# A 2-layer hybrid decoder step on one core: seven-product up-projection in the last chunk of each MLP too, and the last LayerNorm's first half shared with GpSimd

## The reference, cut to what matters

```python
D_MODEL = 1024; D_FF = 4 * D_MODEL
def layer_norm(x, g, b):
    mu = jnp.mean(x, axis=-1, keepdims=True)
    var = jnp.mean(jnp.square(x - mu), axis=-1, keepdims=True)
    return (x - mu) * lax.rsqrt(var + LN_EPS) * g + b
def squared_relu_mlp(x, w_up, w_down):
    return jnp.square(jax.nn.relu(x @ w_up)) @ w_down
...
for i in range(DEPTH):            # layer 0: recurrent mixer, layer 1: attention
    ...
    xp = layer_norm(ALPHA * xp + mp, ln1_g[i], ln1_b[i])
    xs = layer_norm(ALPHA * xs + ms, ln1_g[i], ln1_b[i])
    xp = layer_norm(ALPHA * xp + squared_relu_mlp(xp, mlp_w_up[i], mlp_w_down[i]), ln2_g[i], ln2_b[i])
    xs = layer_norm(ALPHA * xs + squared_relu_mlp(xs, mlp_w_up[i], mlp_w_down[i]), ln2_g[i], ln2_b[i])
```

## Time and profile before

| | us |
|---|---|
| median of three timed runs (1097.07 to 1097.62) | 1097.09 |
| the profiled execution, its own time | 1098.72 |
| its span, first to last instruction | 1096.9 |
| PE busy | 1076.7 |
| DVE busy | 802.6 |
| ACT busy | 562.0 |
| POOL busy | 163.7 |

### The profile page before, as it was taken

The page is one execution under the profiler, slowest core; times in us unless marked ns, Lnnn a source line. Parts: engine busy times, 40 slices in busy tenths (PEclk is TensorE's granted clock), DMA queues, the critical chain, the costliest instruction groups (busy, mean ns, idle before and its releaser), DMA issues.

```text
span 1096.9 us, 22319 instructions
## 1 busy us (share of the span) xinstructions
PE 1076.7 (98%) x8535; PEld 1054.7 (96%) x8535; DVE 802.6 (73%) x1264; ACT 562.0 (51%) x995; POOL 163.7 (15%) x200
## 2 busy tenths in 40 slices
PE   8999999999999999999999999999999999999996
PEld 7999999999999999999999878999999999999996
DVE  6999899896758568566874574789958668586666
ACT  5999857652433425333666775665533424235233
POOL 2343042000000000011243564300000000000023
PEclk9999999999999999999999999999999999999998
DMA  7323224031413314173041221130423403234202
GB/s 248 115 87 97 74 63 136 19 116 58 136 40 133 117 36 134 44 245 101 20 135 45 61 59 38 48 108 1 154 65 110 134 24 129 72 101 135 77 1 82
DMA packets 63709, 98.66 MB, mean 90 GB/s; under 512 B 4384, under 2 KB 44768, under 8 KB 63616
## 3 DMA queue, kind: packets, MB, share of 16 engines
q1 hardware_dynamic: 62944, 94.81, 27.4%
q0 software_dynamic: 400, 2.21, 0.5%
...
q10 hardware_dynamic: 288, 0.59, 0.2%
...
## 4 chain that ended last, share of the span: by engine, by line
PE 80%; DVE 10%; ACT 4%; issue 2%; DMA 1%; POOL 1%; SPq 0%; DVEq 0%; ACTq 0%; POOLq 0%
PE bank L1921 10%; PE bank L1922 9%; PE bank L1923 9%; PE bank L2166 8%; PE bank L2168 8%; PE bank L2167 8%; PE bank L2140 6%; PE bank L2142 6%; PE bank L2141 6%; PE bank L1999 2%; PE bank L2001 2%; PE bank L2000 2%; DVE w_lo L1107 2%; PE bank L2275 1%; PE bank L2300 1%
## 5 line engine op out<-in xcount | busy, mean ns | idle before, releaser
L1114 DVE TENSOR_TENSOR w_lo<-stage,w_hi 128x1024 fp32r<-128x1024 f32 x120 | 144.8, 1219 | 56.1 <-ACT w_hi L648 56.1
L648 ACT ACTIVATE w_hi<-stage 128x1024 fp32r<-128x1024 f32 x120 | 124.4, 1054 | 112.5 <-DVE stage L1132 64.7
L1921 PE MATMUL bank<-x_hi,w_hi 128*128 128x288 f32 (+1 forms) x560 | 163.9, 293 | 1.4 <-issue 0.6
L1922 PE MATMUL bank<-m_lo,w_hi 128*128 128x288 f32 (+1 forms) x560 | 162.2, 290 | 0.0
L1922 PE MATMUL bank<-x_lo,w_hi 128*128 128x288 f32 (+1 forms) x560 | 161.7, 289 | 0.0
L1921 PE MATMUL bank<-m_hi,w_hi 128*128 128x288 f32 (+1 forms) x560 | 161.6, 289 | 0.0
L1923 PE MATMUL bank<-m_hi,w_lo 128*128 128x288 f32 (+1 forms) x560 | 161.6, 289 | 0.0
L1923 PE MATMUL bank<-x_hi,w_lo 128*128 128x288 f32 (+1 forms) x560 | 160.9, 287 | 0.0
L2140 PE MATMUL bank<-m_hi,w_hi 128*128 128x288 f32 (+1 forms) x512 | 147.7, 289 | 0.3 <-DVE m_lo L1457 0.3
L2142 PE MATMUL bank<-m_hi,w_lo 128*128 128x288 f32 (+1 forms) x512 | 147.6, 288 | 0.0
L2141 PE MATMUL bank<-m_lo,w_hi 128*128 128x288 f32 (+1 forms) x512 | 147.4, 288 | 0.0
...
## 6 DMA issues: line engine op xcount, KB each, us to landing
stage<-w_up SPq DMA_DIRECT2D x64, 512.0 KB, 4.4
stage<-w_down SPq DMA_DIRECT2D x64, 512.0 KB, 3.7
stage<-w_qkv SPq DMA_DIRECT2D x10, 512.0 KB, 4.0
stage<-w_x SPq DMA_DIRECT2D x8, 512.0 KB, 5.2
stage<-w_y SPq DMA_DIRECT2D x8, 512.0 KB, 3.6
stage<-w_out SPq DMA_DIRECT2D x8, 512.0 KB, 3.7
stage<-w_o SPq DMA_DIRECT2D x8, 512.0 KB, 3.8
...
```

Of the source, the lines that this page charges most:

```text
L648: A(hi, raw, ACT.Copy).then_inc(s_whi, 1)
L1114: vt.tensor_tensor(lo, raw, hi.bitcast(F32), ALU.subtract).then_inc(s_wlo, 1)
L1921: mm(out, wh, xh, start=(k == 0), stop=False)
L1922: mm(out, wh, xl, start=False, stop=False)
```

## The change

The last chunk (7) of each MLP now uses the seven products too, so chunks 2 to 6 are in the loop. PE's order in it is P1, P2, P6, P5, P3, P7, down half 0, P4, `norm_sums` of half 0, down half 1. P4 is needed for the hidden tiles 0 and 1 of half 1 alone, and down half 1 takes its k steps in the order 2, 3, 0, 1. The banks of these units are now given by hand (the lists in `plan`). The load of the attention's caches by GpSimd waits for P3 of the last chunk of layer 0, since it overwrites s1 and s4. In the last LayerNorm, half 0, DVE subtracts and multiplies for pairs 0 and 1 and GpSimd for pairs 2 and 3 (`last_norm_a`); ACT applies gain and bias to all 8 tiles, where GpSimd took four of them.

```diff
-            plan(("last", l), "A" * 4 + "V" * 8 + "A")
-            plan(("ln", 2 * l + 1, 0), "AV")
-            plan(("last_rest", l), "A" * 3 + "V" * 8)
+            b = [(len(reader) + k) % BANKS for k in range(BANKS)]
+            plan(("last", l), "AA-VAAAA-V-V" + "V" * 8 + "-A",
+                 b[6:8] + b[2:4] + b[6:8] + b[4:6] + b[4:6] + b[6:8] + b[0:6] + b[0:2] + b[6:8])
+            plan(("ln", 2 * l + 1, 0), "AV", b[2:4])
+            plan(("last_rest", l), "V" * 8, b[4:6] + b[0:2] + b[6:8] + b[2:4])
...
+        LAST_AT = {P1: 0, P2: 2, P6: 4, P5: 6, P3: 8, P7: 10, P4: 20}
+        def product_unit(l, c, p, t=0):
+            return chunk_unit(l, c, (LAST_AT[p] if c == CHUNKS - 1 else p) + t)
         def product_done(l, c, p):
-            return chunk_unit(l, c, p) + (4 if p == P4 else 2)
+            return product_unit(l, c, p) + (4 if p == P4 and c < CHUNKS - 1 else 2)
...
-                    elif k % 2 == 0:
-                        A(xhat, xhat, ACT.Identity, bias=b, scale=g).then_inc(s_yout[0], 1)
+                    else:
+                        A(xhat, xhat, ACT.Identity, bias=b, scale=g).then_inc(s_yout[k % 2], 1)
...
+            def last_chunk(l):
+                c, L = CHUNKS - 1, 2 * l + 1
+                t0 = (CHUNKS * l + c) * 8
+                for t in range(2):
+                    keep(l, c, 0, P1, t, h11[:, t, :])
+                split_in(l, c, T3, product_done(l, c, P1))
+                split_in(l, c, B22, product_done(l, c, P2))
+                for t in range(2):
+                    keep(l, c, 0, P6, t, h12[:, t, :])
+                split_in(l, c, T4, product_done(l, c, P6))
+                hidden(l, c, 0, 0, 0, 0, (s_hsq, t0 + 4))
+                for t in range(2):
+                    keep(l, c, 0, P5, t, h22[:, t, :])
+                for k in DOWN:
+                    split_in(l, c, k, down_unit(l, c - 1, 1, 7) + 1)
+                hidden(l, c, 0, 1, 2, 0, (s_hsq, t0 + 6))
+                hidden(l, c, 0, 3, 2, 1, (s_hsq, t0 + 8))
+                for m in range(KT):
+                    square(L, 0, m)
+                act.wait_ge(s_unit, product_done(l, c, P4))
+                b0 = bank_of(product_unit(l, c, P4))
+                A(h21[:, :, :], bank[:, b0:b0 + 2, 0:HW], ACT.Relu).then_inc(s_evA, 1)
+                hidden(l, c, 0, 2, 0, 1, (s_hsq, t0 + 10))
+                norm_stats(L, 0)
+                gj = job_at[("qkv", 0)][0]
+                def beside(t):
+                    if t == 0 and l == 0:
+                        split([gj])
+                    if t >= 2:
+                        square(L, 1, 2 * t - 4)
+                        square(L, 1, 2 * t - 3)
+                norm_apply(L, 0, beside)
...
+                own = 2 if L == 3 else 4
+                for t in range(own):
...
+            def last_up(l):
+                c = CHUNKS - 1
+                split_in(l, c, T3)
+                combine(l, c, 0, P2, h11[:, :, :], P1)
+                relu_sq(l, c, 0, h11[:, :, :], P2)
+                split_in(l, c, B22)
+                hidden_lo(l, c, 0, 0, 0, 0)
+                split_in(l, c, T4)
+                split_in(l, c, D0)
+                split_in(l, c, D1)
+                combine(l, c, 0, P3, h12[:, :, :], P6)
+                relu_sq(l, c, 0, h12[:, :, :], P3)
+                split_in(l, c, D2)
+                split_in(l, c, D3)
+                hidden_lo(l, c, 0, 1, 2, 0)
+                combine(l, c, 0, P7, h22[:, :, :], P5)
+                relu_sq(l, c, 0, h22[:, :, :], P7)
+                hidden_lo(l, c, 0, 3, 2, 1, 2)
+            def last_hidden(l):
+                c = CHUNKS - 1
+                dve.wait_ge(s_evA, read_by(product_unit(l, c, P4, 2), "A"))
+                vt.scalar_tensor_tensor(h21[:, :, :], h21[:, :, :], 0.0, h21[:, :, :], ALU.max, ALU.mult)\
+                    .then_inc(s_hsq, 2)
+                hidden_lo(l, c, 0, 2, 0, 1, 3)
...
-                chunk_up(l, CHUNKS - 2)
-                for m in range(KT):
-                    accumulate(l, CHUNKS - 2, 0, m)
-                    if m >= 4:
-                        split([j7 + m - 4])
-                for m in range(KT):
-                    accumulate(l, CHUNKS - 2, 1, m)
-                for q in range(4):
-                    for k in ((0, 1), (2,), (3,), ())[q]:
-                        split([j7 + 4 + k])
-                    up(l, q, CHUNKS - 1)
+                last_up(l)
                 for m in range(KT):
                     add_tile("down", L, 0, m)
-                up(l, 4, CHUNKS - 1)
+                last_hidden(l)
                 norm_stats(L, 0)
                 gj = job_at[("qkv", 0)][0]
-                def ups(t):
-                    if t == 0:
-                        up(l, 6, CHUNKS - 1)
-
                 def tail(t):
-                    if t == 0:
-                        up(l, 7, CHUNKS - 1)
-                        if l == 0:
-                            split([gj])
+                    if t == 0 and l == 0:
+                        split([gj])
                     if t == 1 or t == 2:
                         add_tile("down", L, 1, 2 * t - 2)
                         add_tile("down", L, 1, 2 * t - 1)
-                norm_apply(L, 0, tail, ups,
-                           after_centre=lambda: up(l, 5, CHUNKS - 1))
+                norm_apply(L, 0, tail)
...
+            def last_norm_a():
+                c0, n = HALF[0]
+                idx = 2 * 3
+                def pair(t):
+                    return acc[:, 2 * t:2 * t + 2, c0:c0 + n]
+                def wide(a):
+                    return a[:, 0:n].rearrange("p (o n) -> p o n", o=1).broadcast_to([128, 2, n])
+                pool.wait_ge(s_evA, read_by(mark[("ln", 3, 0)] + 1, "A"))
+                for t in (2, 3):
+                    seq[0] += 1
+                    pt.tensor_tensor(pair(t), pair(t), wide(mean), ALU.subtract).then_inc(s_seqP, 1)
+                pool.wait_ge(s_seqP, seq[0])
+                pool.wait_ge(s_xhat, 4 * idx + 2)
+                for t in (2, 3):
+                    pt.tensor_tensor(pair(t), pair(t), wide(rstd), ALU.mult).then_inc(s_xhat, 1)
...
-            pool.wait_ge(s_unit, down_unit(0, CHUNKS - 2, 0, 7) + 1)
+            pool.wait_ge(s_unit, product_done(0, CHUNKS - 1, P3))
...
-                for k in range(4):
-                    pe.wait_ge(s_hlo, i * 8 + (t0 + k + 1))
+                for n, k in enumerate((2, 3, 0, 1) if h and c == CHUNKS - 1 else range(4)):
+                    pe.wait_ge(s_hlo, i * 8 + (t0 + n + 1))
...
             def down_bank(l, c, h, m, i):
-                if h == 0 and 0 < c < CHUNKS - 1:
+                if c == CHUNKS - 1:
+                    if h or m > 5:
+                        free_bank(down_unit(l, c, h, m))
+                    else:
+                        pe.wait_ge(s_evV, read_by((chunk_unit(l, c, 0), product_unit(l, c, P2, 2),
+                                                   product_unit(l, c, P3, 2))[m // 2], "V"))
...
-                with pe.Fori(0, CHUNKS - 4) as i:
+                with pe.Fori(0, CHUNKS - 3) as i:
                     chunk_up(l, 2, w0, i)
                     down(l, 2, 0, w0, i)
                     down(l, 2, 1, w0, i)
-                chunk_up(l, last - 1, w0)
-                down(l, last - 1, 0, w0)
-                down(l, last - 1, 1, w0)
-                up(l, last, 0, w0)
+                for p in (P1, P2, P6, P5, P3, P7):
+                    upward(l, last, p, w0)
                 down(l, last, 0, w0)
-                up(l, last, 1, w0, ts=(0,))
+                upward(l, last, P4, w0)
                 norm_sums(2 * l + 1, 0)
-                up(l, last, 1, w0, ts=(1, 2, 3))
                 down(l, last, 1, w0)
             def scores(o):
```

199 lines of the change are left out of this document (78 added, 121 removed).

## The result

| | before | changed |
|---|---|---|
| median of the runs, us | 1097.08 (1097.02 to 1097.62, 4 runs) | 1113.59 (1112.02 to 1114.07, 4 runs) |
| ratio, 95% interval | | 1.0143 [1.0130, 1.0157] |
| profiled run, us: time / span / granted clock | 1098.72 / 1096.9 / 0.996 | 1113.55 / 1111.7 / 0.987 |

The change makes the kernel 16.5 us slower; forecast were 14.0 more, 1111.1 us.

What follows compares the result with a forecast made beforehand. PE, busy 98% of the span, was taken as the bound: matmuls removed -5.65, qkv stop +12.3, clock +2.0, late slabs +3.6, end +1.8, in all +14.05 us, for a median of 1111.1 us, range 1103 to 1117.

Steps and rivals of the forecast that it cites:

- The sign and the cause: Start of qkv in layer 0: PE waits 12.3 us for DVE's add of tile 7, outweighing the 5.65 us removed.
- The clock: First matmuls of qkv in layer 0, behind PE's stop: lower clock level costs 2.0 us, bounds 0 and 5.7.
- The late down slabs: Down half 0 in both last chunks: PE waits for the hidden pair, 2.7 us in layer 0, 0.9 in layer 1.
- The end: Last LayerNorm in layer 1: DVE's add of tile 7 starts after PE is through, 1.8 us lost, bounds 0 and 6.
- The sum: Whole kernel: -5.65 + 12.3 + 2.0 + 3.6 + 1.8 = +14.05 us; forecast median 1111.1 us, 1.3% slower.

Runs made afterwards that it cites:

- bank run: Changed kernel with layer 0's qkv half 0 given the banks of down half 1 tiles 0 to 3 instead of tiles 6, 7, 0, 1; 1106.71 us.
- the run that kept PE busy: Changed kernel with 54 matmuls of ones times ones put on PE between down half 1 and qkv of layer 0; 1112.68 us.
- the other traces of this stop: Three edits of the changed kernel outside layer 0: GpSimd sharing removed, 1111.00 us; sharing moved later, 1109.57; layer 1 and last LayerNorm as before, 1108.44.
- the late sharing: Changed kernel with GpSimd's four last-LayerNorm instructions moved behind its squares, and ACT's scaling of pairs 2 and 3 behind the last square root; 1109.57 us.

## Why the prediction was right, and which terms were not

- **The sign and the cause: right.** PE reached qkv at T+13.8 (T+13.6 in the sum) and waited for DVE's add of tile 7, which ended at T+25.8 (T+25.9). The wait was 12.15 us where 12.3 were reckoned. The bank run shows that it was the bank, and that the order of DVE behind it made it long.
- **The clock: right in kind and size.** 2.0 was taken, between 0 and 5.7. Qkv's first 24 matmuls took 5.12 us instead of 2.83: 2.3 us; the run that kept PE busy gave back 2.2, and by the other traces of this stop it is 1.3 to 1.7. The Trainium skill's rule that PE gaps make the clock fall back and that every stop is paid again (TensorE: Matmul & The Clock Gate, HAM oscillation) agrees with the trace at this place; the last section has stops that were not paid.
- **The late down slabs: the step that failed.** "Its third k step ... needs the hidden pair `h12`. ACT writes its high part behind the splits of the four down slabs": 3.6 us were put down for both layers, and 0.1 came. By the marks A to a and B to b hold nothing but the moved matmuls. ACT's timeline says why: the last two splits started 16.5 and 17.8 us into the chunk, where the looped chunk had 16.7 and 18.9, and the pair's low part on DVE ended at 20.7, before the k step needs it at 20.9. The fourth slab came a microsecond sooner than in the loop, and the caches, the first of them issued 2.2 us behind the last down slab, did not push these: the last two slabs took 3.7 and 4.5 us to land. They pushed the slabs of `w_qkv`, which took 12.1 us in the median and weren't needed yet. I had taken the loop's row as a floor, and the 5.5 us of the earlier trace rows for a price of every slab near the caches. It is the median of 3.7, 4.6, 6.5 and 9.9 us, and the two long ones were issued together with the first cache (484.6) and behind two of them (486.1).

```profile
513.45 1.06 ACT L652 ACTIVATE w_hi<-stage 128x1024 fp32r<-128x1024 f32 x1 [1.99 <-DMA stage<-w_down]
514.69 1.06 ACT L652 ACTIVATE w_hi<-stage 128x1024 fp32r<-128x1024 f32 x1 [0.18 <-DMA stage<-w_down]
...
516.93 0.68 DVE L1519 TENSOR_TENSOR m_lo<-h,m_hi 128x512 fp32r<-128x512 f32 x1
```

- **The end: the mechanism right, its size too small.** 1.8 us were taken and 6.2 came. "The last add starts at T+15.6": it started at T+18.0. Without GpSimd beside it DVE starts it at T+15.2 (the late sharing), so 2.8 us are contention. In the prediction this stood as "some 3 us" beside the sum and under the bound of 6, and the sum went by the case without it, though its own row, 1.30 us for 0.69, said otherwise. Of the 1.8 in the sum itself 1.35 came. The rest is a second fall of the clock, which the sum for the end had at nothing: PE stood 4.36 us, the clock fell 0.5 us behind the add, where it had fallen 4.6 us behind it, and from the add to the matmuls of the diagonal it took 7.5 us instead of 4.9, 2.6 more; 0.6 of them don't show in the 6.2, for the last stretch of the old trace was that much too long. The bound of 6 held the one, and not quite the two together.
- **The sum.** The slabs were 3.5 us too much and the end 4.4 too little, so that the sum, 14.05, came near the 14.8 of the spans by luck as well. The forecast is 2.5 us short of the median: 0.8 by the sum, and 1.6 since the profiled run of before stood that much above its median and the one of after did not; the start of the program alone differs by 1.9 us from run to run.
